# The end of the experts: the last pair's down weights in column halves and another slot, the next gate's first weights in four parts and split earlier

## The reference

```python
hid = jax.nn.silu(a) * b * comb[:, g, :, None]      # 32 experts, width 512, for each expert a, b = t @ w_gate, t @ w_up
y = y + jnp.einsum('tef,efd->td', hid, w_down[g])
...
x = x + y
gate = jax.nn.sigmoid(rmsnorm(x, g_ple) @ w_ple_gate)
x = x + gate * (p @ w_ple_proj)
```

## Time and profile before

| | |
|---|---|
| median of three runs | 1030.92 us (1028.1 to 1031.9) |
| profiled execution | 1029.13 us, of it span 1027.4 us |
| TensorE busy | 955.8 us, 93% |
| VectorE busy | 499.5 us, 49% |
| ScalarE busy | 329.9 us, 32% |
| mean granted TensorE clock | 0.973 |
| HBM read | 287.43 MB |

### The profile page before, as it was taken

The page is one execution under the profiler, slowest core; times in us unless marked ns, Lnnn a source line. Parts: engine busy times, 40 slices in busy tenths (PEclk is TensorE's granted clock), DMA queues, the critical chain, the costliest instruction groups (busy, mean ns, idle before and its releaser), DMA issues.

```text
span 1027.4 us, 14198 instructions
## 1 busy us (share of the span) xinstructions
PE 955.8 (93%) x5926; PEld 679.4 (66%) x5926; DVE 499.5 (49%) x870; ACT 329.9 (32%) x525; POOL 37.8 (4%) x39
## 2 busy tenths in 40 slices
PE   5999799999999999998999799699988989999997
PEld 5997535443444444443433689678888989999885
DVE  6684513132222222232221675968887567676642
ACT  5722211100001000000010654546556545545531
POOL 1000000000000000000000000232220000000000
PEclk9999799999999999999999899799999989999999
DMA  9947699999999999999999822442333524445401
GB/s 360 417 191 300 273 377 424 417 430 429 430 432 429 428 432 431 429 429 432 430 430 426 333 83 83 164 164 82 132 115 120 207 105 148 181 168 200 167 1 41
DMA packets 23621, 289.45 MB, mean 282 GB/s; under 512 B 2560, under 2 KB 4864, under 8 KB 6016
## 3 DMA queue, kind: packets, MB, share of 16 engines
q1 hardware_dynamic: 22832, 286.91, 68.0%
q10 hardware_dynamic: 720, 1.57, 0.4%
HBM read 287.43 MB, written 1.05 MB: 281 GB/s over the span
## 4 chain that ended last, share of the span: by engine, by line
PE 77%; DVE 11%; DMA 4%; ACT 4%; issue 3%; SPq 0%; DVEq 0%; ACTq 0%
PE ps L270 76%; DVE wl L266 4%; DMA arena<-in_moe 4%; DVE arena L1456 2%; ACT wh L259 1%; PE ps L959 1%; DMA vec<-in_vec 0%; DVE arena L547 0%; DVE arena L352 0%; ACT arena L1762 0%; ACT in_h L617 0%; DVE arena L1084 0%; DVE arena L1669 0%; DVE arena L1805 0%; ACT arena L1765 0%
## 5 line engine op out<-in xcount | busy, mean ns | idle before, releaser
L270 PE MATMUL ps<-ring,arena 128*64 128x512 f32 x1232 | 340.1, 597 | 7.8 <-issue 7.8
L270 PEld LDWEIGHTS ps<-ring,arena 128*64 128x64 f32 x1232 | 108.9, 137 | 168.0 <-issue 165.7
L266 DVE TENSOR_TENSOR wl<-ring,wh 128x1024 fp32r<-128x1024 f32 x150 | 180.9, 1237 | 62.5 <-ACT wh L259 62.5
L270 PE MATMUL ps<-arena 128*64 128x512 f32 (+4 forms) x432 | 163.9, 530 | 10.6 <-DVE arena L1633 9.0
L259 ACT ACTIVATE wh<-ring 128x1024 fp32r<-128x1024 f32 x150 | 151.3, 1050 | 28.5 <-PE ps L270 23.9
L1070 DVE SCALAR_TENSOR_TENSOR arena<-ps,arena 128x512 f32<-128x512 f32 x16 | 12.0, 751 | 214.4 <-PE ps L270 214.4
L270 PEld LDWEIGHTS ps<-arena 128*64 128x64 f32 (+2 forms) x432 | 57.8, 147 | 57.6 <-issue 42.6
L270 PE MATMUL ps<-up_h,wh 128*128 128x256 f32 x352 | 88.4, 286 | 4.6 <-DVE up_l L1886 4.6
L270 PE MATMUL ps<-up_l,wh 128*128 128x256 f32 x352 | 87.9, 285 | 0.0
L270 PE MATMUL ps<-h_h,wh 128*128 128x256 f32 x256 | 67.5, 296 | 3.7 <-DVE wl L266 2.5
L270 PEld LDWEIGHTS ps<-up_h,wh 128*128 128x128 f32 x352 | 67.6, 192 | 5.0 <-issue 4.9
(11 more groups left out here) (262 smaller groups left out, 1523.4 us busy)
## 6 DMA issues: line engine op xcount, KB each, us to landing
ring<-in_moe SPq DMA_DIRECT2D x77, 2048.0 KB, 21.3
arena<-in_moe SPq DMA_DIRECT2D x19, 2048.0 KB, 26.0
ring<-in_w_in SPq DMA_DIRECT2D x12, 2048.0 KB, 9.1
ring<-in_w_up SPq DMA_DIRECT2D x11, 2048.0 KB, 8.0
ring<-in_w_dn SPq DMA_DIRECT2D x5, 2048.0 KB, 7.9
ring<-in_w_out SPq DMA_DIRECT2D x4, 2048.0 KB, 15.2
ring<-in_w_pg SPq DMA_DIRECT2D x2, 2048.0 KB, 22.4
ring<-in_w_in SPq DMA_DIRECT2D x2, 1024.0 KB, 8.8
```

The lines of the kernel that those rows point to most:

```text
L266: e.tensor_tensor(wl(i), raw_piece(i), wh(i), SUB).then_inc(*lo.up(i))
L270: return e.matmul(o, l, r, start=first, stop=final, skip_group_check=True)
```

## The change

The last pair's d31 goes to slot 5, as its place in the list says, and no longer to slot 4. Both down matrices of the last pair are loaded in column halves: first columns 0 to 511 of each of the four row blocks for both experts, then 512 to 1023; the first halves count up the semaphore `s_half`, the second the slots' own. `down(15)` waits for the first halves ahead of n = 0 and for the whole matrices ahead of n = 1. `pgate` 0 is packed piece by piece in HBM and loaded in four parts, with a semaphore for each (three of them are ones of the first loads of the kernel, which stand at 16 by then). Pieces 0 and 1 are split behind the eviction of half 0 of the last pair, 2 and 3 behind that of half 1; on VectorE pieces 0 and 1 between the two remainders, piece 2 between the additions of half 0 and those of half 1, and piece 3 behind all additions. In `four`, called with `first`, the low pieces are waited for behind the pass over the high ones, and used in a pass of their own.

```diff
         for i in range(len(order)):
             k = SLOTS[0][i] if i < N0 else SLOTS[1][(i - N0) % 10] if i < N1 else SLOTS[2][(i - N1) % 4]
-            if i == N1 - 1:
-                k = 4
...
             if name == "fdn":
                 return w[:, j * 1024:j * 1024 + 1024]
+            if name == "pgate":
+                return piece_view(w[:, j * 1024:j * 1024 + 1024], name)
...
                 if i == 2:
                     e.wait_ge(s_half, 16)
+                elif (name, m) == ("pgate", 0) and j < 3:
+                    e.wait_ge(l_part[j], 32)
+                elif (name, m) == ("pgate", 0):
+                    e.wait_ge(*loaded(name, m))
                 elif j == 0:
                     e.wait_ge(*loaded(name, m))
...
             for j in range(4):
                 e.wait_ge(*hi.at(i0 + j))
-                e.wait_ge(*lo.at(i0 + j))
+                if first is None:
+                    e.wait_ge(*lo.at(i0 + j))
             if first is not None:
                 for c in range(8):
                     e.wait_ge(*first.at(c))
                     for j in range(4):
                         mm(e, outs[j], wh(i0 + j)[:, c, :], xh[:, c, :], c == 0, False)
+                for j in range(4):
+                    e.wait_ge(*lo.at(i0 + j))
+                    for c in range(8):
                         mm(e, outs[j], wl(i0 + j)[:, c, :], xh[:, c, :], False, False)
...
             def down(q):
                 wv = [slot("d", 2 * q + r).rearrange("p (c n) -> p c n", c=4) for r in range(2)]
-                e.wait_ge(*loaded("d", 2 * q))
-                e.wait_ge(*loaded("d", 2 * q + 1))
+                if q == NP - 1:
+                    e.wait_ge(s_half, 48)
                 e.wait_ge(*b4.at(q))
                 for n in range(2):
+                    if n or q < NP - 1:
+                        e.wait_ge(*loaded("d", 2 * q))
+                        e.wait_ge(*loaded("d", 2 * q + 1))
...
                 else:
+                    split_lo(e, FIRST + 2)
                     rest(q, 1)
                     add(q, 0)
+            split_lo(e, FIRST + 3)
             add(NP - 1, 1)
...
                     e.activation(parted(q, n)[0][:, :], ps[5 + n][:, :], ACT.Copy).then_inc(*yh.up(q, n))
+                    if q == NP - 1:
+                        split_hi(e, FIRST + 2 + 2 * n)
...
         def ple_act(e):
-            split_hi(e, FIRST + 4)
-
-        def ple_act_2(e):
...
+                if (name, n) in (("d", NE - 2), ("d", NE - 1)):
+                    halves.append([v.rearrange("p (f n) -> p f n", f=4) for v in (dst, src)])
+                    e.dma_start(halves[-1][0][:, :, 0:512], halves[-1][1][:, :, 0:512]).then_inc(s_half, 16)
+                    if n == NE - 1:
+                        for (a, b), to in zip(halves, (ring_sem[place[i - 1][0]], ring_sem[k])):
+                            e.dma_start(a[:, :, 512:1024], b[:, :, 512:1024]).then_inc(to, 16)
+                elif (name, n) == ("pgate", 0):
+                    for j in range(4):
+                        sl = slice(j * 1024, j * 1024 + 1024)
+                        e.dma_start(dst[:, sl], src[:, sl]).then_inc(l_part[j] if j < 3 else ring_sem[k], 16)
...
-    r["w_pg"] = _cols(i["w_ple_gate"][0], 2)
+    r["w_pg"] = np.ascontiguousarray(i["w_ple_gate"][0].reshape(8, 128, 2, 4, 128).transpose(2, 1, 3, 0, 4)).reshape(2, 128, -1)
```

More of the change, by code:

```diff
@@ L357, in build @@
         s_out = sem("s_out")
+        l_part = [l_xT, l_vec, l_xk]
         XT = A(0, 8, 256)
@@ L1351, in ple_dve @@
             split_lo(e, FIRST + 4)
-        def ple_dve_2(e):
             for c in range(8):
@@ L2065, in loads @@
             e.dma_start(vec[:], dr["vec"]).then_inc(l_vec, 16)
+            halves = []
             for i, (name, n) in enumerate(order):
@@ L2079, in loads @@
                     e.wait_ge(*proj.at("in1", 4, 3))
-                if i == 0:
+                if (name, n) in (("d", NE - 2), ("d", NE - 1)):
[8 more added lines that the diff above has]
+                        e.dma_start(dst[:, sl], src[:, sl]).then_inc(l_part[j] if j < 3 else ring_sem[k], 16)
+                elif i == 0:
                     dst, src = (v.rearrange("p (c n) -> p c n", c=8) for v in (dst, src))
@@ L2120, in _ @@
             ple_dve(e)
-            ple_dve_2(e)
             in2_dve(e)
@@ L2135, in _ @@
             ple_act(e)
-            ple_act_2(e)
             in2_act(e)
```

## The result

The changed kernel takes 1026.74 us (median of 18 runs, 1025.15 to 1029.05), the kernel before 1030.53 in 18 runs beside it: ratio 0.9958, interval 0.9946 to 0.997. That is 3.8 us by the medians and 4.3 by the ratio; 7.2 were forecast. The time lies inside the range, but with 0.42% the case that came was "within 0.5%", to which I had given 0.21.

What follows compares the result with a forecast made beforehand. TensorE, 93% busy, was taken to bound the kernel, idling 5.8 us for VectorE's fourth subtraction. 5.6 us of earlier start plus 1.6 us of clock gave 7.2 us: 1030.92 to 1023.7 us, range 1020.5 to 1028.

Steps and rivals of the forecast that it cites:

- within 0.5%: Case for the whole kernel: measured time within 0.5%, or 5.2 us, of the kernel before; chance 0.21.
- What bounds: End of the experts: TensorE's 5.8 us wait for low halves of a weight split, ended last by VectorE's fourth subtraction.
- Slot 5 instead of 4: Loads of the last pair: the gate's first four pieces go into slots 4 and 6, both free by 536.86.
- the eviction n=1 started later than 566.6: Sign of being wrong, at the last pair's second eviction on ScalarE: a later start would mean late parts.
- late parts: Rival at the piece loads and down(15)'s n=1: parts cost some or all gain, chance 0.04; enough to be slower, 0.02.
- later stretches: Rival after the gate: half-clock stretches, such as that from 663.7, change and cost up to 3.5 us; chance 0.11.
- The split moved in ahead: ScalarE and VectorE around the last evictions: pieces 0 and 1 split early, n=1 not delayed, ple_h from 568.95 instead of 570.84.
- The order of the matmuls: Gate's matmuls on TensorE: high pass needs only ple_h, so begins at 569.5 instead of 575.06, 5.6 us earlier.
- The clock: Gate's first 17 matmuls: a gap of some 0.2 us instead of 5.8 keeps the clock up; 1.6 us come back.
- my rival: Gate's first passes: the clock falls anyway, fed step by step by ScalarE, costing 1.6 to 3.2 us; chance 0.16.
- Down halves: Loads of d30 and d31: halves gain nothing, short runs land the gate's matrix 0 to 1.6 us later, 1 taken.
- Parts and additions: Gate's parts issued at 536.86, landing 560.7 to 564.4; VectorE's third subtraction ahead of additions 2 and 3 makes ple_h wait.

Runs made afterwards that it cites:

- e4: The kernel before with only the new order inside the gate's first four, low pass behind the high one: 1026.62 us, ratio 0.9958.
- e1: The changed kernel with d31 back in slot 4, all else kept: 1022.79 us, ratio 0.9931.
- e3: The changed kernel with d31 back in slot 4 and d30 and d31 loaded whole again: 1022.2 us, ratio 0.9921.
- e6: The kernel before with 48 added matmuls of unused result behind the last scatter, in TensorE's idle time: 1027.92 us, ratio 0.9966.
- e10: The kernel before with the last down matrices in column halves and nothing else: 1030.35 us, ratio 0.9991.
- e7: e3 with the gate's first matrix in one load and one wait instead of four parts: 1023.43 us, ratio 0.9918.
- e9: e3 with VectorE's third subtraction behind all additions: 1023.89 us, ratio 0.9922.
- e5: The changed kernel with all four splits back behind the last eviction and VectorE's four subtractions behind all additions: 1026.49 us, ratio 0.9948.
- e8: e1 with the last down matrices in column quarters, eight loads with runs of 1 KB: 1022.74 us, ratio 0.9922.
- e2: The changed kernel with d30 and d31 loaded whole again, d31 still in slot 5: 1027.7 us, ratio 0.9966.

## Why the prediction was half right

**What bounds.** Right. VectorE's fourth subtraction ended the wait; e4 takes only this away and brings 5.2 us in its profile.

**Slot 5 instead of 4.** This step failed: "Now slot 4's last tenant is u29 and slot 6's is d28", so that the split could begin at 563.7. The places turn at 28 modulo 8 = 4, the split needed slots 5 and 7, and d31 held slot 5 until the last down matmul. What the prediction listed as the sign of being wrong, "the eviction n=1 started later than 566.6", did show, but not from late parts: the wait stood in front of the splits for another reason. Its price: 1.95 us in the eviction n=1 (5.39 against 3.44), 0.4 us more until the gate's start (in the changed kernel 3.44 us behind n=1, in e1 3.03), and 1.4 us in the clock (16.28 against 14.84). Sum 3.8, the difference between 25.11 and 21.30. VectorE has its part in the 0.4 us: its first two subtractions, late with the splits, stood in front of the remainder, which began 1.46 us behind n=1 (571.98 against 570.52) where in e1 it began 0.64 us behind it.

That the time lies in the range all the same is luck as far as this step goes. The upper end came from two rivals on the clock, 3.2 us for the gate's matmuls and 3.5 for later stretches; what came cost 3.8 us against e1, and only 1.4 of it was clock. No rival had the slot in it.

**The split moved in ahead.** Right once the slot is right. With slot 4 the gate starts 5.48 us earlier (11.94 to 6.46) where 5.6 were forecast, and the scaling comes 7.1 us earlier (28.39 to 21.30) where 7.2 were. By their ratios, 0.9931 and 0.9921, e1 and e3 gained 7.1 and 8.1 us, by their medians 8.3 and 8.9.

**The order of the matmuls.** Right in mechanism; not separated in the sum. It holds 3.6 of the 5.5 us of earlier start, and the early split, on top of it, the other 1.9.

**The clock.** The term of 1.6 us was right in size (e6). That the gap would be 0.2 us was right with slot 4 (0.3). In the changed kernel the gap was 3.2 us and the clock fell: my rival came true, behind a wait ahead of the scatter and not through ple_h's slow steps.

**Down halves.** Worth almost nothing, and harmless. The forecast of no gain at all, because the eviction of the transposes covers the landing, was off by 0.15 us, and in e3 the landing did come last. My 1 us for the short runs was of the right size: d31's last half landed at 547.48 + 14.6 = 562.1 where the old trace, moved by 2.2 us, has 560.7. Missed entirely: an issue that blocks SyncE for 18 us. e1 beside e3, and e10, show that it cost nothing; the transfers went on meanwhile, in the changed kernel at 429 GB/s from 514 to 541 and at 407 from 541 to 556.

**Parts and additions.** The parts are worth nothing measurable (e7), the third subtraction's place neither (e9). "Issued at 536.86 as before" was wrong by 12 us, without effect.

**Behind the scaling.** The distance from the scaling to the span's end is 435.9 us before and 436.7 in the changed kernel, 434.6 in e1 and 435.4 in e3: over all profiled executions it lies between 434.2 (e9) and 437.2 (e5), within what the rival on later stretches allowed. e3 is the fastest by its median; it is not separated from e1, e7, e8 or e9.

## What to carry to other kernels

When pieces turn around a ring, work out the place of the piece in question with its number before you say which slot frees it; a wait ahead of a moved step is then found in a line of arithmetic, and not in the profile. A step that is moved into an engine's idle time must have all of its inputs and its destination free at the beginning of that idle time, otherwise it turns idle time off the path into a wait on it, here 1.95 us with a low clock behind. And try the cheapest part of a bundle alone: the order of one loop nest held as much as the whole change as it was made.

## What the runs showed of the hardware

An issue on SyncE's queue can block for long: with the down matrices in halves (runs of 2 KB) the issues took 0.6, 5.5, 18.2 and 3.7 us, and in e2, whole (runs of 16 KB), 0.33 and 0.43. In e10 one took 17.8 us without any other part of the change. It comes with the short runs and not with the number of loads: in e2 the gate's four parts, with runs of 4 KB, took 1.75 us for all four. Older loads were in flight in every case, so whether that is needed isn't shown, nor is a limit behind it.

The same idle time gave both levels of the clock: 2.21 us ahead of the gate in e4 with 1.00 behind it, 2.22 us in e5 with 0.50 from 0.6 us behind the gate's first matmul on. No fall came behind the gaps of 0.2 to 0.4 us in e1, e3, e7, e8 and e9; one came with each of the four gaps of 3.2 and 5.8 us (changed kernel and e2, kernel before and e10), in e2, e10 and the kernel before still in the gap, in the changed kernel 1.0 us after its end. 48 matmuls with no use in the gap kept it up, for 1.6 us of gain in the profiled stretch.
